# Moved work at four places of two attention mixers in a one-core transformer kernel: loads of the start, a convolution, an output block and query blocks

## The reference, cut to what matters

```python
def gdn_mixer(hn, w_in, conv_w, a_log, dt_bias, o_gain, w_out):
    proj = hn @ w_in
    qkv, z, b_raw, a_raw = jnp.split(proj, ...)
    qkv = jax.nn.silu(causal_depthwise_conv(qkv, conv_w))
    q, k, v = jnp.split(qkv, [GDN_KDIM, 2 * GDN_KDIM], axis=-1)
    q, k = l2_norm(heads(q)), l2_norm(heads(k))
    o = gated_delta_rule(q, k, v, beta, g)
    o = rms_norm(o, o_gain) * jax.nn.silu(zf)
    return o @ w_out

def sb_mixer(hn, k_sh, v_sh, w_q, q_gain, w_out):
    q = rms_norm(hn @ w_q, q_gain)
    z = q @ k_sh.T * scale
    ls_neg = log_sigmoid(-z)
    log_fail = where(causal, ls_neg, 0)
    log_a = z + ls_neg + reverse_cumsum(log_fail) - log_fail
    o = where(causal, exp(log_a), 0) @ v_sh
    return o @ w_out
```

## Time and profile before

| | us |
|---|---|
| median of 3 runs | 2262.6 (2261.05 to 2262.95) |
| the profiled execution, its own time | 2260.11 |
| its span in the profile | 2258.0 |
| TensorE matmul busy | 2211.8 (98% of the span) |
| VectorE busy | 1113.1 |
| ScalarE busy | 928.7 |
| GpSimd busy | 286.7 |

### The profile page before, as it was taken

The page is one execution under the profiler, slowest core; times in us unless marked ns, Lnnn a source line. Parts: engine busy times, 40 slices in busy tenths (PEclk is TensorE's granted clock), DMA queues, the critical chain, the costliest instruction groups (busy, mean ns, idle before and its releaser), DMA issues.

```text
span 2258.0 us, 28381 instructions
## 1 busy us (share of the span) xinstructions
PE 2211.8 (98%) x11050; PEld 1811.5 (80%) x11050; DVE 1113.1 (49%) x1411; ACT 928.7 (41%) x1255; POOL 286.7 (13%) x247
## 2 busy tenths in 40 slices
PE   7999999999999999998999999999999999999998
PEld 5788888788888888876888888888788788888887
DVE  6665656354443233454444432355665655555522
ACT  5444554243222234565322222255565564444312
POOL 0111112210000110001300001100000035222211
PEclk9999999999999999999999999999999999999999
DMA  3311111122223222201222322321111213222221
GB/s 135 113 57 38 54 41 38 57 94 93 93 97 106 95 86 82 77 36 38 93 93 95 107 96 93 124 108 68 62 61 56 71 52 136 93 93 94 103 101 56
DMA packets 31629, 185.39 MB, mean 82 GB/s; under 512 B 3104, under 2 KB 7584, under 8 KB 11184
## 3 DMA queue, kind: packets, MB, share of 16 engines
q1 hardware_dynamic: 29520, 176.46, 22.4%
q0 software_dynamic: 2016, 7.60, 1.0%
HBM read 179.83 MB, written 7.37 MB: 83 GB/s over the span
## 4 chain that ended last, share of the span: by engine, by line
PE 93%; DVE 3%; ACT 2%; issue 1%; DMA 0%; SPq 0%; POOL 0%; DVEq 0%; POOLq 0%
PE ps L1794 25%; PE ps L1796 25%; PE ps L1795 25%; PE ps L2025 4%; PE ps L2497 1%; PE ps L2440 1%; PE ps L2480 1%; PE ps L2507 1%; PE ps L2280 1%; PE ps L2046 1%; PE ps L2318 1%; PE ps L1982 0%; PE ps L2438 0%; PE ps L2079 0%; PE ps L2099 0%
## 5 line engine op out<-in xcount | busy, mean ns | idle before, releaser
L1794 PE MATMUL ps<-xh,wh 128*128 128x512 f32 x1888 | 764.6, 405 | 4.5 <-DVE xl L1247 2.9
L1796 PE MATMUL ps<-xh,wl 128*128 128x512 f32 x1888 | 737.9, 391 | 0.0
L1795 PE MATMUL ps<-xl,wh 128*128 128x512 f32 x1888 | 736.6, 390 | 0.0
L356 ACT ACTIVATE wh<-raw 128x2048 fp32r<-128x2048 f32 x143 | 273.8, 1914 | 543.7 <-PE ps L1796 543.4
L954 DVE TENSOR_TENSOR wl<-raw,wh 128x2048 fp32r<-128x2048 f32 x143 | 331.1, 2316 | 315.7 <-ACT wh L356 315.7
L1794 PEld LDWEIGHTS ps<-xh,wh 128*128 128x128 f32 x1888 | 355.8, 188 | 83.0 <-issue 13.9
L1796 PEld LDWEIGHTS ps<-xh,wl 128*128 128x128 f32 x1888 | 354.9, 188 | 76.2
L1795 PEld LDWEIGHTS ps<-xl,wh 128*128 128x128 f32 x1888 | 355.9, 189 | 70.8 <-issue 4.8
L1794 PE MATMUL ps<-hid_h,wh 128*128 128x512 f32 (+1 forms) x550 | 211.9, 385 | 0.0
L1796 PE MATMUL ps<-hid_h,wl 128*128 128x512 f32 (+1 forms) x550 | 210.6, 383 | 0.0
L1795 PE MATMUL ps<-hid_l,wh 128*128 128x512 f32 (+1 forms) x550 | 208.7, 379 | 0.0
(11 more groups left out here) (362 smaller groups left out, 2847.0 us busy)
## 6 DMA issues: line engine op xcount, KB each, us to landing
raw<-in_stream SPq DMA_DIRECT2D x159, 1024.0 KB, 4.8
hankd<-tabd SPq DMA_DIRECT2D x1, 3072.0 KB, 17.5
hank<-hankd POOLq DMA_DIRECT2D x4, 768.0 KB, 5.0
hT<-in_xT SPq DMA_DIRECT2D x4, 512.0 KB, 5.4
keepd<-hT POOLq DMA_DIRECT2D x1, 2048.0 KB, 10.0
hT<-keepd POOLq DMA_DIRECT2D x8, 256.0 KB, 5.2
out<-hT SPq DMA_DIRECT2D x8, 256.0 KB, 2.6
raw<-in_stream SPq DMA_DIRECT2D x2, 512.0 KB, 7.5
```

What stands on the lines that cost most here:

```text
L356: act.activation(wh[:, s, :], raw[:, s, :], ACT.Copy).then_inc(hi_made, 1)
L1794: pe.matmul(out, w_hi, a_hi, start=start, stop=False)
L1795: pe.matmul(out, w_hi, a_lo, start=False, stop=False)
L1796: return pe.matmul(out, w_lo, a_hi, start=False, stop=stop)
```

## The change

It has seven parts.

- The load of `ones` is issued alone, directly behind the first part of `x`; `ident` is loaded behind the second unit, counted in the semaphore of the tables, and TensorE waits for all three of those tables before its first transposes with `ident` instead of a little later.
- In the period of head 0 the convolution of head 1's q stands behind `inverse_t(p, 2)`.
- At the end of the first mixer the output chunks 4 to 7 use banks 6, 7, 4, 5, and four of chunk 4's eight blocks run before the wait for input chunk 7. For the unit that they need, VectorE runs both halves of `lo_half` ahead of `scale_out`.
- In the second mixer the query blocks of heads 2 and 3 stand behind head 0's scores, head 3's in bank 4 (so head 0's `rest` waits until it is copied), and head 0's `q_sums` goes into the middle of head 1's block.
- The copies of heads 2 and 3 (`q_in`, `q_squares`) both stand in step 1.
- VectorE scales head 0's q before it copies head 1's and before it splits the next unit.
- In step 6 ScalarE rounds four chunks instead of five at first; the fifth and the unit (`split_hi`, and VectorE's `split_lo`) follow behind that step's softplus.

```diff
@@ -69,0 +70 @@
+OUT_BANK = {n: (0, 1, 2, 3, 6, 7, 4, 5) if n == "gdn_out" else range(8) for n in ("gdn_out", "sb_out", "mix_out")}
@@ -87,2 +88,3 @@
-Q_IN_AT = {2: 0, 3: 1, 4: 3, 5: 4, 6: 5, 7: 6}
-Q_DENSE_AT = {0: (3, 0, 8), 1: (4, 0, 4), 2: (4, 4, 8), 3: (5, 0, 8), 4: (6, 0, 8), 5: (7, 0, 8)}
+Q_IN_AT = {2: 1, 3: 1, 4: 3, 5: 4, 6: 5, 7: 6}
+Q_BANK = {1: 5, 3: 4}
+Q_DENSE_AT = { 1: (4, 0, 4), 2: (4, 4, 8), 3: (5, 0, 8), 4: (6, 0, 8), 5: (7, 0, 8)}
@@ -308,0 +311,2 @@
+                if k == 1:
+                    sp.dma_start(mats[:, MAT["ones"], :], io["mats"][:, MAT["ones"], :]).then_inc(ones_in, 16)
@@ -310 +313,0 @@
-            sp.dma_start(mats[:, 0:2, :], io["mats"][:, 0:2, :]).then_inc(ones_in, 16)
@@ -316,0 +320 @@
+            sp.dma_start(mats[:, 0, :], io["mats"][:, 0, :]).then_inc(tab_in, 16)
@@ -747 +751 @@
-                if t >= 6:
+                if t >= 7:
@@ -749,2 +753,2 @@
-                if t in (1, 4, 6):
-                    split_hi(u0 + 3 + (1, 4, 6).index(t))
+                if t in (1, 4):
+                    split_hi(u0 + 3 + (1, 4).index(t))
@@ -754,0 +759,3 @@
+                if t == 6:
+                    fill_chunk(om_sb, 4, om_sb_made, 0)
+                    split_hi(u0 + 5)
@@ -1013 +1020 @@
-                    dve.tensor_tensor(hT[:, c, :], hT[:, c, :], ps[:, c, :], ALU.add).then_inc(resid_added, 1)
+                    dve.tensor_tensor(hT[:, c, :], hT[:, c, :], ps[:, OUT_BANK[name][c], :], ALU.add).then_inc(resid_added, 1)
@@ -1283,2 +1289,0 @@
-                else:
-                    conv_q(1, range(4))
@@ -1285,0 +1291,2 @@
+                if p == 0:
+                    conv_q(1, range(4))
@@ -1330 +1336,0 @@
-            scale_out(HEADS - 1, 5)
@@ -1331,0 +1338 @@
+            scale_out(HEADS - 1, 5)
@@ -1373 +1380 @@
-            q_bank = lambda h: 5 if h == 1 else 0
+            q_bank = lambda h: Q_BANK[h] if h in Q_BANK else 0
@@ -1421,2 +1427,0 @@
-                if t == 6:
-                    split_lo(u0 + 5)
@@ -1424,0 +1430,2 @@
+                if t == 6:
+                    split_lo(u0 + 5)
@@ -1427,2 +1433,0 @@
-            split_lo(u0 + 1)
-            q_in(1)
@@ -1429,0 +1435,2 @@
+            q_in(1)
+            split_lo(u0 + 1)
@@ -1911 +1918 @@
-                m = three(ps[:, c, :], wh[:, s, w], wl[:, s, w], xh[:, kc, :], xl[:, kc, :], kc == 0, kc == KC - 1)
+                m = three(ps[:, OUT_BANK[name][c], :], wh[:, s, w], wl[:, s, w], xh[:, kc, :], xl[:, kc, :], kc == 0, kc == KC - 1)
@@ -1916 +1923 @@
-            def out_rest(name, first=6):
+            def out_rest(name, first=6, begun=0):
@@ -1927 +1934 @@
-                    for kc in range(KC):
+                    for kc in range(begun if c == 4 else 0, KC):
@@ -1953,0 +1961 @@
+            pe.wait_ge(tab_in, 48)
@@ -1960 +1967,0 @@
-            pe.wait_ge(tab_in, 32)
@@ -2172 +2179,5 @@
-            out_rest("gdn_out", 7)
+            unit_ready(U0["gdn_out"] + 2)
+            pe.wait_ge(ti_made, 4 * HEADS)
+            for kc in range(4):
+                out_block("gdn_out", 4, kc)
+            out_rest("gdn_out", 7, 4)
@@ -2245 +2256 @@
-                elif h == 1:
+                elif h in Q_BANK:
@@ -2249 +2260 @@
-                s, bank = (u0 + h // 2) % 2, 5 if h == 1 else 0
+                s, bank = (u0 + h // 2) % 2, Q_BANK[h] if h in Q_BANK else 0
@@ -2300,0 +2312,2 @@
+                else:
+                    pe.wait_ge(q_copied, 4)
@@ -2321,4 +2334,4 @@
-            for h in range(3):
-                q_dense(h)
-                if h == 1:
-                    q_sums(0)
+            q_dense(0)
+            q_dense(1, 0, 4)
+            q_sums(0)
+            q_dense(1, 4, 8)
@@ -2330,0 +2344,3 @@
+                if t == 0:
+                    q_dense(2)
+                    q_dense(3)
```

More of the change, by code:

```diff
@@ L1282, in period @@
                     lo_half(2 * p + 3, 0)
-                else:
+                inverse_t(p, 2)
+                if p == 0:
                     conv_q(1, range(4))
-                inverse_t(p, 2)
                 if last:
@@ L1329, in _ @@
             lo_half(U0["gdn_out"] + 2, 0)
+            lo_half(U0["gdn_out"] + 2, 1)
             scale_out(HEADS - 1, 5)
-            lo_half(U0["gdn_out"] + 2, 1)
             dve.wait_ge(o_scaled, HEADS)
@@ L1420, in step @@
                 q_scale(t + 1)
+                remainder(t - 1)
+                softplus(t)
                 if t == 6:
                     split_lo(u0 + 5)
-                remainder(t - 1)
-                softplus(t)
             q_in(0)
+            q_scale(0)
+            q_in(1)
             split_lo(u0 + 1)
-            q_in(1)
-            q_scale(0)
             split_lo(u0 + 2)
```

## The result

| | before | changed |
|---|---|---|
| median of 4 runs, us | 2262.19 | 2245.72 |
| lowest and highest, us | 2261.05, 2262.95 | 2245.10, 2246.26 |
| the profiled execution, us | 2260.11 | 2246.26 |
| its span, us | 2258.0 | 2244.1 |

The changed kernel is faster: the ratio is 0.9929, with a 95% interval from 0.9916 to 0.9942. Between the medians lie 16.5 us, between the two profiled executions 13.9, since the one of before (2260.11) was faster than its four timed runs and the one of the change was its slowest.

The account below looks back on a forecast made before the run. TensorE's queue was taken as the bound, so only its waits and lower-clock work could be gained: 2.0 + 0.9 + 4.05 + 4.3 + 5.1 = 16.35 us. From 2262.6 that gave 2246.3 us, range 2243 to 2255.

Parts of the forecast that it names:

- What bounds the kernel: Whole kernel: TensorE's queue, busy 2211.8 of 2258.0 us; only its waits and lower-clock work can be gained.
- The start: Program start: `ones` loaded earlier lets ScalarE's norm start at 13.2, not 15.24; 2.0 us, bounds 1.4 and 2.1.
- The first head: Head 0, first mixer: wait for `T` falls from 1.75 to about 0.1, convolution waits 0.8; 0.9 us gained.
- The output block: End of first mixer: four blocks of chunk 4 cover the 2.69 us wait and the clock stays up; 4.05 us.
- The query blocks: Second mixer, head 0: earlier scores remove the 2.53 us wait for `la` and 1.8 of half clock; 4.3 us.
- The late split: Second mixer, step 6: the wait for weights falls from 3.93 to 0.5 us, plus 1.7 of clock; 5.1 us.
- The clock's terms: Half-clock stretches behind three removed waits, first mixer's end and second mixer: 1.35 + 1.8 + 1.7 us, called not sure.
- The sum: Whole kernel: 2.0 + 0.9 + 4.05 + 4.3 + 5.1 = 16.35 us gained, giving 2246.3 us.
- (a): Whole kernel: clock not regained, other short idle stretches bring slow stretches back; gain 11.5 us, 2251.1; chance 0.15.
- (b): Second mixer: its waits return in another form, ScalarE or VectorE being late; gain 6.9 us, 2255.7; chance 0.07.
- (c): Whole kernel: nothing measurable, the places being paid for by a later unseen wait; 2262.6 us; chance 0.04.
- (d): Second mixer's steps: slower, the chain from norm to weights outlasting TensorE's work; 2267.1 us; chance 0.02.

Follow-up runs that it names:

- the start alone: Kernel before with only the load of `ones` behind x's first part, `ident` later and the wait for the tables changed; 2260.08 us against 2262.25.
- the first mixer alone: Kernel before with only the convolution and the output block of the first mixer moved; 2254.32 us, ratio 0.9965.
- the query blocks alone: Kernel before with only the second mixer's query blocks of heads 2 and 3, their copies and VectorE's order moved; 2257.50 us, ratio 0.9983.

## Why the prediction was right, and where it was not

The predicted 2246.3 us lie 0.6 us from the measured 2245.72, inside the range from 2243 to 2255. By its steps:

- **What bounds the kernel** held: TensorE's busy time hardly changed, and what was gained at each place was still there at the end (13.98 at the last place, 13.9 at the end).
- **The start**: the forecast was 2.0 us, with 1.4 as the lower bound, and this step failed. The changed kernel's trace shows 0.6 us at the norm (14.63, where 13.2 were forecast) and -0.45 us at the second `U`; over all profiles it is about 0.7. Three terms were wrong. "Issuing `ones` between the parts takes at most the 0.58 us of today's issue" took the cost of the issue for the cost of the place: the second square came 2.0 us later (7.75 against 5.75) and the last 0.94, so the last input was there at 12.30 and not by 11.95. "The last product costs 5.28 / 4 = 1.3 us on average" took the mean of products at both paces for one that now runs at the slower: the sum came 2.3 us behind its input, which is the larger part of the miss. And "I leave its 1.5 us where it is" left out that the clock's fall could come ahead of the work: 5.93 us of work, not 3.0, were at the lower clock, and a lead of 0.62 us at the first dense product (18.37 against 18.99) became a lag of 0.45 at the second `U`. That one is a matter of the execution: with the same start, the start alone has 2.8 us of work at the lower clock. That the norm would be held by ScalarE's own rounding came true only where the load was taken away (12.02, no idle time).
- **The first head**: forecast 0.9, measured 0.92. The new wait for the convolution is 0.51 us by the profile and not 0.8. The step named the right place for it.
- **The output block**: forecast 4.05, measured 4.0. The unit and chunk 7 were both in time.
- **The query blocks**: forecast 4.3, measured 4.5. `la` from 940.03 to 941.52 is 2.9 us ahead of TensorE's 944.41, where 3 were forecast; q is ready at 929.51, 0.4 us ahead of the scores, as worked out. The unit's split ends at 933.02, 0.44 us ahead of the block that needs it (933.46), where 0.8 were forecast, so the cover was thinner than the sum had it.
- **The late split**: forecast 5.1, measured 5.0; the wait left is 0.47 us, forecast 0.5.
- **The clock's terms** hold as sizes in this pair of traces, and filling the idle stretches in the kernel before gave 4.9 us (2.9 to 7.0), which is their sum of 1.35 + 1.8 + 1.7. They are not fixed costs, though: in the profiles of the start alone and of the first mixer alone the wait for `la` cost no clock, and in that of the query blocks alone the wait of step 6 cost more. The prediction cited the Trainium skill, page "TensorE: Matmul & The Clock Gate" (The HAM clock gate), where it says that the monitor runs freely and does not start with the kernel. The traces agree: the stretch behind one and the same 2.53 us wait is there in one execution and missing in another, and at the start it takes in 3.0 us of work in one and 5.93 in another.
- **The sum** came out right partly because errors met. In the profiles the gain is 13.9 us, 2.45 under the forecast 16.35, and that is the start's miss. The medians give 16.5. The kernel before has more idle stretches behind which the clock can fall, so its typical execution may lose more than the profiled one, which was faster than all four timed runs; that this makes the other 2.6 us is argued and not shown, since no trace of a slower execution of it was taken. That the forecast lies within 0.6 us is thus in part luck.
- **The rivals**: (a), the clock not regained, would have left the slow stretches at the three places; none is there, nor anywhere else between 25 and 2239 us. (b) would have shown a wait of TensorE in the second mixer for a unit or for q; there is none. (c) and (d) are excluded by the time.

The version that beats both kernels is the changed one with `ones` written by VectorE and the idle stretch behind the norm's sum filled: 2241.15 us.

## What to carry to other kernels

A wait of the bounding engine is worth its length plus what the clock loses behind it. The second part differs from execution to execution, so one profile does not price it; it can be measured by itself over many runs, and was won back here, with products that nobody reads in the idle stretch. When work is moved out from before a late result, look at once for what is moved into its place: here the convolution behind `T` took back about half of the 1.75 us. And at the start the place of a small load among the large ones mattered more here than its bytes (1.4 to 2.0 us for the place, 0.2 to 0.7 for twice the bytes): a constant can be written by an idle engine and needs no load at all. Last, an average over products at two paces is no price for the one product that ends last.

## What the runs showed of the hardware that was not expected

- A load of 64 KB issued by SyncE between two loads of 512 KB made the part behind it land 1.4 to 2.0 us later in three traces (second square at 7.21, 7.57 and 7.75 against 5.73 to 5.85 in the eight with no load there); 128 KB in the same place 2.2 us (7.91). Issued from ScalarE's queue, half a us earlier, it made the first two squares 0.5 us later (4.94 and 6.26 against 4.48 and 5.73), and the last no later than in one of the two runs without a load (9.02 against 8.71 and 9.82).
- The same idle stretch of TensorE, 2.53 us, was followed by 3.60 us at the lower clock in the kernel before and by none in the kernels with only the start or only the first mixer changed. Behind one of 3.8 us at the start, the work at the lower clock was 3.00 us before, 2.8 in the start alone, 5.16 to 5.20 with `ones` from ScalarE's queue and with the first mixer alone, and 5.93 in the changed kernel, where the clock fell about 1 us ahead of the work.
- Products without use stood in four idle stretches, and in these profiles no half-clock stretch followed any of the four. For the one of 2.53 us this proves little, since two profiles have none there without them.
- In the first products of the program the two matmuls of an fp32 product lie about 0.85 us apart (0.81 in the changed kernel) or 0.43 (before), while the column of the granted clock reads 1.00 at both paces.
